# Query and gate tiles of a hybrid encoder layer: six of the second half's eight pairs by seven products of quarters

## What is computed

```
z = rms_norm(h, norm_gain)
proj = einsum("bld,de->ble", z, w_in)            # 1024 -> q 1024, k 128, v 128, g_attn 1024, u_pool 1024, g_pool 1024
q, k = partial_rotary(q), partial_rotary(k)      # first 16 of 64 dims of each head
o_attn = chunked_window_attention(q, k, v, sinks)   # own chunk of 64, the one before, the meta tokens
o_pool = multiscale_pool_mixer(u_pool, w_pool, pool_scale)
gated = concat([silu(g_attn) * o_attn, silu(g_pool) * o_pool])
h = h + einsum("ble,ed->bld", gated, w_out)
return rms_norm(h, final_norm_gain)[:, 16:]
```

## Time and profile before

| | us |
|---|---|
| median of 3 runs (lowest, highest) | 1247.1 (1245.3, 1247.57) |
| the profiled execution | 1246.68 |
| its span | 1244.9 |
| PE busy | 1229.7 (99%) |
| DVE busy | 779.5 (63%) |
| ACT busy | 575.0 (46%) |
| POOL busy | 178.0 (14%) |
| stage A of the second half ends (its first `scores`) | 850.1 |

### The profile page before, as it was taken

One profiled execution on the slowest core, in us unless ns is written; L12 is line 12 of the kernel. 1 busy time (PEld: TensorE's weight loads), 2 busy tenths in 40 slices (PEclk: granted clock), 3 DMA queues, 4 the chain that ended last, 5 costly groups with the idle time before them and its releaser, 6 DMA issues.

```text
span 1244.9 us, 16835 instructions
## 1 busy us (share of the span) xinstructions
PE 1229.7 (99%) x6077; PEld 996.8 (80%) x6077; DVE 779.5 (63%) x1240; ACT 575.0 (46%) x1362; POOL 178.0 (14%) x178
## 2 busy tenths in 40 slices
PE   9999999999999999999999999999999999999997
PEld 9788888877777777888888888887777777788886
DVE  6553645557575756957776544436766676695757
ACT  6622222255555555444665222224555555544445
POOL 1154655600000002000011211111000000200000
PEclk9999999999999999999999999999999999999999
DMA  9525444411111112823352211111111111253324
GB/s 358 205 85 169 135 152 135 139 47 35 34 34 35 34 34 86 325 96 119 101 200 71 85 52 49 51 51 34 34 34 52 34 34 35 70 218 102 118 87 167
DMA packets 34153, 122.60 MB, mean 98 GB/s; under 512 B 3568, under 2 KB 3600, under 8 KB 34096
## 3 DMA queue, kind: packets, MB, share of 16 engines
q1 hardware_dynamic: 21408, 74.98, 18.0%
q0 software_dynamic: 12688, 46.83, 10.5%
HBM read 100.83 MB, written 20.97 MB: 98 GB/s over the span
## 4 chain that ended last, share of the span: by engine, by line
PE 95%; DVE 2%; ACT 1%; DMA 1%; issue 0%; DVEq 0%; SPq 0%; ACTq 0%
PE ps L1125 20%; PE ps L1126 19%; PE ps L1127 19%; PE ps L1369 7%; PE ps L1371 7%; PE ps L1370 7%; PE ps L1284 3%; PE ps L1341 2%; PE ps L1319 2%; PE ps L1343 1%; PE ps L1167 1%; PE ps L1136 1%; PE ps L1191 1%; PE ps L1192 1%; PE ps L1193 1%; DMA xr<-in_x 1%
## 5 line engine op out<-in xcount | busy, mean ns | idle before, releaser
L1125 PE MATMUL ps<-zh,wsplit 128*128 128x512 f32 x1072 | 421.7, 393 | 0.1
L1127 PE MATMUL ps<-zh,wsplit 128*128 128x512 f32 x1072 | 417.8, 390 | 0.0
L1126 PE MATMUL ps<-zl,wsplit 128*128 128x512 f32 x1072 | 417.6, 390 | 0.0
L783 DVE TENSOR_TENSOR wsplit<-wraw,wsplit 128x1024 fp32r<-128x1024 f32 x124 | 186.7, 1506 | 102.9 <-ACT wsplit L511 102.9
L1127 PEld LDWEIGHTS ps<-zh,wsplit 128*128 128x128 f32 x1072 | 201.2, 188 | 42.6
L1126 PEld LDWEIGHTS ps<-zl,wsplit 128*128 128x128 f32 x1072 | 201.5, 188 | 40.3
L1125 PEld LDWEIGHTS ps<-zh,wsplit 128*128 128x128 f32 x1072 | 201.4, 188 | 40.4 <-DVE wsplit L783 0.5
L1369 PE MATMUL ps<-wsplit,gsh 128*128 128x512 f32 x448 | 174.6, 390 | 1.9 <-DVE gsl L1030 1.7
L511 ACT ACTIVATE wsplit<-wraw 128x1024 fp32r<-128x1024 f32 x124 | 132.4, 1067 | 91.4 <-PE ps L1371 75.1
L1370 PE MATMUL ps<-wsplit,gsh 128*128 128x512 f32 x448 | 174.3, 389 | 0.0
L1371 PE MATMUL ps<-wsplit,gsl 128*128 128x512 f32 x440 | 171.2, 389 | 0.0
(11 more groups left out here) (160 smaller groups left out, 1329.6 us busy)
## 6 DMA issues: line engine op xcount, KB each, us to landing
wraw<-in_wa SPq DMA_DIRECT2D x36, 512.0 KB, 3.5
wraw<-wt SPq DMA_DIRECT2D x32, 512.0 KB, 3.3
wraw<-in_wq SPq DMA_DIRECT2D x24, 512.0 KB, 3.7
tq<-in_wq POOLq DMA_DIRECT2D x8, 1024.0 KB, 6.2
wt<-tq POOLq DMA_DIRECT2D x8, 1024.0 KB, 5.1
wraw<-wc SPq DMA_DIRECT2D x16, 512.0 KB, 3.3
wraw<-in_wb SPq DMA_DIRECT2D x16, 512.0 KB, 3.3
rows<-in_x POOLq DMA_DIRECT2D x16, 512.0 KB, 10.4
```

The lines of the kernel that those rows point to most:

```text
L783: ve.tensor_tensor(wl[:, slot, 0:size], wraw[:, slot, 0:size], wh[:, slot, 0:size].bitcast(F32), ALU.subtract).then_inc(w_lo, 1)
L1125: te.matmul(ps[:, PB[bank], :], w_h, rhs_z(zh, tb, k), start=k == 0, stop=False)
L1126: te.matmul(ps[:, PB[bank], :], w_h, rhs_z(zl, tb, k), start=False, stop=False)
L1127: last = te.matmul(ps[:, PB[bank], :], w_l, rhs_z(zh, tb, k), start=False, stop=k == KT - 1)
```

## The change

In the second half the pairs j = 2..7 (`PAIR0 = 2`) are no longer two tiles of 48 matmuls each. Query and gate tile of a pair are taken together as a product of a 1024 x 1024 input (two halves of tokens, two halves of features) with a 1024 x 256 weight (two halves of features, query and gate columns), and computed in Strassen's way in the form of Winograd: seven products of quarters, each 4 slices of features times 3 passes, 12 matmuls of 512 columns, 42 products in all. Products 1, 3, 5 and 7 of a pair go to one PSUM bank, 4 to a second and 2 and 6 to a third; pairs alternate between banks 0 to 2 and 3 to 5.

What it needs:

- **Weight sums**, made in the first half by POOL: for each of the pairs 2 to 7 it loads the pair's two tiles (`ta_q`, `ta_g`), makes four subtractions, and stores four quarters in DRAM (`wat`); after the last pair it copies the 18 quarters that need no sum from DRAM to DRAM. `ta_g` lies where `probs` does, so the first exponentials of the first half wait for the stores.
- **Input sums** `s1` to `s4` of quarters of the input (2048 columns each), made in the second half by DVE (six sums in all, with `s1f` to `s4f` rebuilt from `zh` + `zl`), copied to their high parts by ACT (four copies of 2048 columns) and subtracted to their low parts by DVE (four). They lie in the upper half of `gates` and in the region of `tq`; the fourth takes the place of a quarter of `zh` and `zl`, which goes to DRAM (`za`) before and comes back after the products.
- Because the upper part of `gates` is taken, **the gates of pairs 0 to 6** of the second half go through one tile `gstage` to DRAM (`gd`, 512 KB a pair, on SP's queue), and come back in four parts before and in stage B. The next pair's first write to `gstage` waits for the store (`g_out`).
- A weight block now holds two quarters and serves two products, so the pairs 2 to 7 take 22 blocks in place of 12, each split by ACT and DVE as before.
- PSUM is read out between products: ACT copies products 1, 2 and 3 (to `qk`, `gstage`, `qk`), DVE adds products 4 and 6 to them into `rotsrc` and product 5 into `gstage`; then shuffle, sine, cosine and rotate as before, and the gates from tanh of `gstage` and of product 7's bank.

The core of the diff (bookkeeping of block and use counts left out):

```diff
@@ POOL, first half, pair j
+                    if h == 0 and j >= PAIR0:
...
+                            pool.wait_ge(ta_out, 16 * 4 * (j - PAIR0))
+                        gp.dma_start(ta_q[:, :, :], wa[2 + 2 * j].rearrange("p (q n) -> p q n", n=TB)).then_inc(ta_in, 16)
+                        gp.dma_start(ta_g[:, :, :], wa[3 + 2 * j].rearrange("p (q n) -> p q n", n=TB)).then_inc(ta_in, 16)
                     times_cos((1 + HT) * h + 1 + j)
...
+                    if h == 0 and j >= PAIR0:
+                        b12, b22, b11, b21 = (part[:, q, :] for part in (ta_g, ta_q) for q in range(2))
+                        pool.wait_ge(ta_in, 32 * (j - PAIR0 + 1))
+                        for i, (o, a, b) in enumerate(((b11, b12, b11), (b12, b22, b12), (b22, b22, b11), (b21, b21, b22))):
+                            gp.tensor_tensor(o, a, b, ALU.subtract).then_inc(ta_step, 1)
+                            pool.wait_ge(ta_step, 4 * (j - PAIR0) + i + 1)
+                        for there, part in ((T1_AT, b11), (T3_AT, b12), (T2_AT, b22), (T4_AT, b21)):
+                            gp.dma_start(wat_at(j, there), part).then_inc(ta_out, 16)
+                if h == 0:
+                    for j in range(PAIR0, HT):
+                        for there, tile, rows_half in ((B11_AT, 2 + 2 * j, 0), (B21_AT, 2 + 2 * j, 1), (B22_AT, 3 + 2 * j, 1)):
+                            gp.dma_start(wat_at(j, there), wa[tile, :, rows_half * TB:rows_half * TB + TB]).then_inc(wat_out, 16)
@@ ACT
+                    for q in range(NPROD):
+                        jj, i = divmod(q, PRODUCTS)
+                        j = PAIR0 + jj
+                        if i < 3:
+                            act.wait_ge(x_done, q + 1)
+                            if i == 1:
+                                act.wait_ge(g_out, 16 * j)
+                                sc.activation(gate_tile_at(h, j)[:, TB:2 * TB], s_bank(j, i), ACT.Copy).then_inc(x_copy, 1)
+                            else:
+                                sc.activation(to_pair(j, i // 2), chunks(s_bank(j, i)), ACT.Copy).then_inc(x_copy, 1)
...
+                        if q in LAST_OF and BLOCK_OF[q] + 2 <= NBLK:
+                            split_s(BLOCK_OF[q] + 2)
+                        if q == 1:
+                            act.wait_ge(za_out, 32)
+                            act.wait_ge(pb_done[1], USES * h + 2 * PAIR0 + 2)
+                            sum_hi(quarter(zh, 1, 0), s1f, 8)
+                        if q == 2:
+                            act.wait_ge(q_lo, 3)
+                            sum_hi(s4h[:, :, :, :], s4f, 8)
...
+                if h == 0:
+                    act.wait_ge(ta_out, 16 * 4 * (HT - PAIR0))
                 exponents(NCH * h)
@@ DVE
+                    SUMS = [((0,), (1,), (2, 3, 4)), ((5,), (7,), (6, 8))]
+                    for j in range(PAIR0):
+                        pair_a(j, [[s_sums[i] for i in places] for places in SUMS[j]])
+                    split_lo(block_s(1), 1)
+                    for q in range(NPROD):
...
+                        if i == 0 and jj > 0:
+                            rotate(r - 1, qk[:, :, j, :])
+                        if i in (3, 5):
+                            half = i // 4
...
+                            ve.tensor_tensor(chunks(rotsrc[:, half * TB:half * TB + TB]), chunks(s_bank(j, i)),
+                                             qk[:, half * NCH // 2:(half + 1) * NCH // 2, 1 + j, :], ALU.add).then_inc(rot_in, 1)
+                            if half:
+                                swap(r)
...
+                        if q in LAST_OF and BLOCK_OF[q] + 2 <= NBLK:
+                            b = BLOCK_OF[q] + 2
+                            split_lo(block_s(b), b % 2, (BLOCK_OF.count(b) or 2) * TB)
...
+                    rotate((1 + HT) * h + HT, qk[:, :, HT, :])
@@ PE
+                    for q in range(NPROD):
+                        jj, i = divmod(q, PRODUCTS)
+                        pe.wait_ge(w_lo, block_s(BLOCK_OF[q]) + 1)
...
+                        if i in (2, 4, 5):
+                            pe.wait_ge(x_copy, 3 * jj + {2: 1, 4: 3, 5: 2}[i])
+                        if i == 6:
+                            pe.wait_ge(x_gate, jj + 1)
+                        if jj == 0 and i in (1, 2, 4, 6):
+                            pe.wait_ge(q_lo, {1: 1, 2: 2, 4: 3, 6: 4}[i])
...
+                            te.matmul(s_bank(j, i), w_h, z_h[:, :, k, :], start=S_ANEW[i] and k == 0, stop=False, skip_group_check=True)
+                            te.matmul(s_bank(j, i), w_h, z_l[:, :, k, :], start=False, stop=False, skip_group_check=True)
+                            last = te.matmul(s_bank(j, i), w_l, z_h[:, :, k, :], start=False, stop=k == 3, skip_group_check=True)
+                        last.then_inc(x_done, 1)
```

255 lines of the change are left out of this document (231 added, 24 removed).

## The result

| | before | after |
|---|---|---|
| median (lowest, highest), us | 1247.11 (1245.3, 1247.57) | 1289.35 (1288.06, 1294.08) |
| ratio, 95% interval | | 1.0348 [1.032, 1.0377] |
| span of the profiled execution | 1244.9 | 1286.3 |
| mean granted clock of TensorE, share of full | 0.998 | 0.985 |
| `scores` of the first half, from the second on, later by | | 20.3 |

The change costs 42.2 us. I had forecast 22.5, with 1288.0 as the upper end: the direction was right, the size was not, and the median lies 1.35 us outside the range.

What follows compares the result with a forecast made beforehand. PE was taken to bound the kernel (busy 1229.7 of 1244.9 us). -16.3 + 4.4 + 0.6 + 7.9 + 8.1 + 6.5 + 7.3 + 4 = +22.5 on 1247.1 gave 1269.6 us, range 1251 to 1288.

Steps and rivals of the forecast that it cites:

- Matmuls, -16.3: Second half's pairs: 504 matmuls in place of 576, 72 fewer at 0.227 us each, 16.3 us less.
- Pair 0, 4.4: Second half, pair 0: PE waits 4.4 us, since three DVE sums (6.8) meet 2.4 of cover.
- 0.6: Second half, behind pair 0's silus: ACT's sum copies delay the next tile's split, PE waits 0.6 us.
- First pair, 2.3 + 4.0 + 1.6: First pair's products: PE waits 2.3 us at product 3, 4.0 at product 5 (gate store), 1.6 until product 7.
- Pairs 3 to 7, 8.1: Second half, pairs 3 to 7: late DVE splits and gate stores alternate, 8.1 us of waits in five pairs.
- End of stage A, 6.5: Second half, before `scores`: only product 7 (2.7) covers the last rotation's 9.2 us, so PE waits 6.5.
- First half, 7.3: First half: POOL's last weight store lands at 257.2, delaying the exponentials, so `turn_meta` starts about 7.3 us later.
- 18 copies ... nothing: First half: POOL's 18 DRAM copies (9.7 us) cost nothing, or 3 us if an issue costs 0.7.
- The clock, 4: After the waits of 6.5 and 7.3 us PE runs slowly: 2 us each, 4 in all, between 0 and 10.
- POOL becomes the bound: Rival, chance 0.15: first half, late stores; PE waits about 2 us before query tiles, 10 at stage B; 1282.
- the clock's rival: Rival, chance 0.15: the clock falls in every wait of 4 us or more, four with 5 us each; 1285.
- The waits are covered: Rival, chance 0.07: pairs 0 to 7 lose nothing, end of stage A 2.9, first half 7.3; 1241.0 us, faster.

Runs made afterwards that it cites:

- run 9: Changed kernel, with ACT copying product 2 behind product 3's copy and split, and DVE splitting ahead of its shuffle: 1270.23 us.
- run 11: Changed kernel with all edits that gained (those of run 5, Run 6, run 7 and run 9 among them) and run 10's: 1250.25 us.
- run 14: run 11 with one silu of the last pair made before product 7's end: 1249.32 us.
- run 12: run 5 with unused matmuls (18, 11, 16, 26) in four waits of its second half: 1270.11 us.
- run 7: Changed kernel with DVE's ten sums of the second half put into its idle times: 1284.09 us.
- Run 6: Changed kernel with the store of pair 1's gates issued one block sooner on SP: 1283.01 us.
- run 5: Changed kernel with the first half's weight sums one pair earlier and the 18 DRAM copies behind attention: 1278.1 us.
- run 3: Changed kernel with the first half's weight sums made one pair earlier: 1279.27 us.
- run 13: Changed kernel with only ACT's copy of product 2 moved behind product 3's copy and split: 1273.72 us.
- run 10: Changed kernel with the last DVE split of the second half's stage A behind the last rotate: 1289.84 us.
- run 2: Changed kernel with 122 unused matmuls filling PE's five longest waits: 1284.08 us.
- run 4: Changed kernel with the 18 copies from DRAM to DRAM put behind attention: 1287.65 us.
- run 17: run 14 with products ordered 1, 4, 3, 2, 5, 6, 7, block 1 split sooner, 12 unused matmuls before `scores`, POOL's cosine ahead of its wait and loads: 1240.8 us.

## Why the forecast was right in direction and wrong in size

By its own steps, forecast and measured in us:

- **Matmuls, -16.3.** 72 fewer with 0.227 between starts, as said. -13.1 by the account, small gaps counted. In runs 9, 11 and 14, with fewer waits, it is -15.2 to -15.3, so 2 of the missing 3 come with the waits; one part is that the first start behind a wait is followed after 0.31 and not 0.227 (run 12, 749.90 to 750.21), some 1 us in 13 waits. The rest I have not settled.
- **Pair 0, 4.4:** 4.29; run 7 removed it by order alone. **0.6** behind it did not come.
- **First pair, 2.3 + 4.0 + 1.6:** 2.66 + 2.60 + 1.21. Run 6 confirms the store as the cause. But 2.60 is low because half clock had made PE 3.1 us late just ahead of it. In run 5, with 1.7 lost there, the wait was 4.00, and in run 3, with nothing lost there, 5.56:

```profile
753.01 0.77 PE L1594 MATMUL ps<-zh,wsplit 128*128 128x512 f32 x1 [5.56 <-DVE zl L1152]
```

  So the 4.0 was 1.6 too small, and that it does not show in the change is the clock's doing.
- **Pairs 3 to 7, 8.1:** 10.7 in eight waits. Both causes right (run 13 and run 9), each a little dearer.
- **End of stage A, 6.5:** 6.07. The reading "a split 1.1, two silus" was right as a queue; run 10 shows that taking out one does not help while another operation with two SBUF inputs stands in the cosine's time.
- Together the second half's waits: 27.5 forecast, **27.5 measured**. The places and their causes are right. That the sums are the same is luck: 0.6 + 4.0 + 8.1 were 0 + 2.6 + 10.7, and with the half clock filled away the waits come to 30.3 (run 2, filled ones counted).
- **First half, 7.3:** 13.45 at `turn_meta` and 2.15 before two query tiles. This is the step that failed, in two places. "The last store is issued at 253.7": it was 261.2. POOL fell 3.4 us behind in its first such pair, where I had 2, and its next four lasted 22.2 to 22.9 and not 21.8, which is 3.9 more. In them it waited 2.5 to 3.0 for the stores where I took 2.2, and up to 1.7 for `tq`, whose load stands behind the four stores and which I had not followed to its landing. From POOL's first and last such pair:

```profile
127.08 3.36 POOL L510 TENSOR_TENSOR rotsrc<-rotsrc,cos_t 128x1024 f32<-128x1024 f32 x1 [3.49 <-DVE swapped L1062]
...
151.18 0.54 POOL L559 DMA_DIRECT2D ta_q<-in_wa  x1 [2.88 <-DMA wat<-ta_q]
...
152.26 2.41 POOL L510 TENSOR_TENSOR rotsrc<-rotsrc,cos_t 128x1024 f32<-128x1024 f32 x1
...
243.21 2.40 POOL L510 TENSOR_TENSOR rotsrc<-rotsrc,cos_t 128x1024 f32<-128x1024 f32 x1
...
247.33 2.66 POOL L567 TENSOR_TENSOR tq<-tq 128x512 f32<-128x512 f32 x2 [1.71 <-DMA tq<-in_wq]
```

  So the last cosine starts at 243.2, not 237, 0.8 of it from the start. "It falls 2 us behind and then about keeps pace" took too little for the first pair, and left out that being late by a little more in every pair adds up. And "18 copies ... nothing": I followed only the keys' copy behind them, not the `memset` ahead of it, which ACT needs before it can copy for `turn_meta`. By run 4 the stores alone give 9.1 for the 7.3, and the `memset` 4.3 where I had nothing. The 7.3 was not clean either: its own terms, 257.2 + 3.0 + 1.0 against 254.99, give 6.2.
- **The clock, 4:** 3.5 + 6.6 = 10.1. The rule I had cited (*TensorE: Matmul & The Clock Gate*, Part 1, of the Trainium skill: half clock after idleness) agrees with this trace: four falls to 1.2 GHz, each in or just behind a wait. What failed is "I take 2 for each wait" of two. Those two took 3.5 and 1.8; two shorter waits, of 4.29 and 2.66 us, had half clock too, 1.7 and 3.1. The rival had four with 5 each. But 10.1 is not what the clock adds to the time: since waits behind it get shorter, filling the waits gained 5.3 (run 2).

Of the 18.9 between 22.5 and 41.4: 6.2 at `turn_meta`, 2.2 at query tiles, 6.1 clock, 3.2 matmuls, 1.3 start and rounding; the first half has 11.0 of it. The stated range was too narrow by the forecast's own working: "with all long ones +45" is 1292, above the 1288 at which I closed it. Of the rivals, "POOL becomes the bound" was half true: PE did wait before query tiles, 1.3 and 0.9 where it said 2 in each, and it waited 13.45 where it said 10, but for other reasons than stores landing in 5.1: they landed in 2.9. Its 1282 and the 1285 of the clock's rival are each nearer than my 1269.6, and both happened at once, which no case of mine had. "The waits are covered" was not so. That its figure, 1241.0, is run 17's time is a coincidence: it had 7.3 in the first half and -13.4 in the second, and run 17 has 1.1 and -6.6, with other edits.

## What to carry to other kernels

When work is put on a queue that was idle, follow everything behind it in that queue, the memset as well as the big copy, and compare the pair's sum with PE's period after the waits for its own DMAs: a little too long is paid as many times as there are pairs. Where an engine in order waits for a DMA, put that wait behind what others need next: one copy moved two places gave back 15 us here, 10.6 of them waits. And price a change that trades matmuls for waits with the clock in it, at several waits and not only the longest, and by runs, since with the same instructions half clock was 7 to 12 us from version to version.
